# Waits of VectorE and ScalarE in the seven-product stages: for each operation's own data instead of for the engine's last instruction

## The reference

```python
h = _rmsnorm(x, norm1_g) * (1.0 + scale1) + shift1
proj = h @ w_in                       # [1024, 1024] @ [1024, 4352]: queries, keys, values, gates
...
h2 = _rmsnorm(x, norm2_g) * (1.0 + scale2) + shift2
u = h2 @ w_up                         # [1024, 1024] @ [1024, 5632]
a, g = jnp.split(u, 2, axis=-1)
a = ap[:, 0:s] * conv_w[0] + ap[:, 1:s + 1] * conv_w[1] + ap[:, 2:s + 2] * conv_w[2] + conv_b
x = x + gate2 * ((gelu(a) * g) @ w_down)
```

## Time and profile before

| | |
|---|---|
| Median of 3 runs | 2711.78 us (2709.85 to 2713.63) |
| The profiled execution | 2708.78 us, span of its trace 2707.0 us |
| TensorE (PE) busy | 2585.8 us, 96% |
| VectorE (DVE) busy | 1528.0 us, 56%, 2083 instructions |
| ScalarE (ACT) busy | 1104.7 us, 41%, 1865 instructions |
| GpSimd (POOL) busy | 856.5 us, 32%, 627 instructions |
| Mean granted TensorE clock | 0.984 |
| U_IN2's steps on TensorE | from 1325.09 to about 1624 us |
| U_FFN's steps on TensorE | from 2040.29 to about 2449 us |

### The profile page before, as it was taken

One profiled execution on the slowest core, in us unless ns is written; L12 is line 12 of the kernel. 1 busy time (PEld: TensorE's weight loads), 2 busy tenths in 40 slices (PEclk: granted clock), 3 DMA queues, 4 the chain that ended last, 5 costly groups with the idle time before them and its releaser, 6 DMA issues.

```text
span 2707.0 us, 34684 instructions
## 1 busy us (share of the span) xinstructions
PE 2585.8 (96%) x12391; PEld 2150.7 (79%) x12391; DVE 1528.0 (56%) x2083; ACT 1104.7 (41%) x1865; POOL 856.5 (32%) x627
## 2 busy tenths in 40 slices
PE   6999999999899999999899997899997999999998
PEld 3888887888787799987678887778875888887887
DVE  5665755630434566657864437866578777771112
ACT  5200002611410688856544437761365555550000
POOL 2233331032233566630222220243002232324664
PEclk8999999999999999999999999999998999999999
DMA  6344444263365544434253337514342333339833
GB/s 245 99 143 134 146 132 125 86 209 102 133 206 167 129 110 109 110 123 156 76 186 133 109 119 185 181 61 148 89 142 81 109 109 109 109 115 310 287 95 119
DMA packets 377272, 374.81 MB, mean 138 GB/s; under 512 B 36323, under 2 KB 284556, under 8 KB 376972
## 3 DMA queue, kind: packets, MB, share of 16 engines
q1 hardware_dynamic: 346844, 303.91, 37.9%
q10 hardware_dynamic: 30256, 68.69, 6.8%
HBM read 286.55 MB, written 85.98 MB: 138 GB/s over the span
## 4 chain that ended last, share of the span: by engine, by line
PE 74%; DVE 13%; ACT 5%; DMA 3%; issue 2%; SPq 1%; POOL 1%; ACTq 0%; DVEq 0%; POOLq 0%
PE PS L1793 28%; PE PS L1878 20%; PE PS L1947 8%; PE PS L811 5%; PE PS L789 2%; DMA mod_raw<-in_w_ada 1%; PE PS L2018 1%; PE PS L1837 1%; PE PS L775 1%; PE PS L774 1%; DVE opBf L3017 1%; DVE Xr L2998 1%; ACT opBf L2161 1%; PE PS L1860 1%; ACT opA L2165 1%
## 5 line engine op out<-in xcount | busy, mean ns | idle before, releaser
L1793 PE MATMUL PS<-opA,w_hi 128*128 128x512 f32 x2176 | 678.7, 391 | 3.0 <-POOL w_lo L1596 3.0
L1793 PEld LDWEIGHTS PS<-opA,w_hi 128*128 128x128 f32 x2176 | 410.0, 188 | 88.8 <-POOL w_lo L1596 3.4
L1793 PE MATMUL PS<-opA,w_lo 128*128 128x512 f32 x1088 | 424.6, 390 | 0.0
L1591 POOL CAST w_hi<-w_raw 128x1024 fp32r<-128x1024 f32 (+1 forms) x117 | 125.1, 1069 | 784.6 <-PE PS L1793 456.7
L1878 PE MATMUL PS<-opB,Xr 128*128 128x512 f32 x1120 | 309.8, 394 | 15.4 <-ACT M L2341 14.7
L1596 POOL TENSOR_TENSOR w_lo<-w_raw,w_hi 128x1024 fp32r<-128x1024 f32 (+1 forms) x118 | 284.8, 2413 | 35.0 <-ACT w_hi L2220 25.6
L1878 PE MATMUL PS<-opA,Xr 128*128 128x512 f32 x980 | 276.2, 392 | 6.6 <-DVE M L3034 3.0
L1878 PEld LDWEIGHTS PS<-opB,Xr 128*128 128x128 f32 x1120 | 212.8, 190 | 61.9 <-ACT M L2341 16.0
L2676 DVE SCALAR_TENSOR_TENSOR M<-mod_raw,small,M 128x512 f32<-128x512 f32 x168 | 181.0, 1077 | 142.7 <-DMA mod_raw<-in_w_ada 82.2
L1793 PEld LDWEIGHTS PS<-opA,w_lo 128*128 128x128 f32 x1088 | 205.1, 189 | 42.4 <-issue 0.2
L1878 PEld LDWEIGHTS PS<-opA,Xr 128*128 128x128 f32 x980 | 182.2, 188 | 50.7 <-ACT M L2341 8.7
(11 more groups left out here) (266 smaller groups left out, 4757.4 us busy)
## 6 DMA issues: line engine op xcount, KB each, us to landing
mod_raw<-in_w_ada SPq DMA_DIRECT2D x96, 256.0 KB, 2.9
z_dram<-opB ACTq DMA_DIRECT2D x44, 512.0 KB, 3.9
w_raw<-in_a_w_in SPq DMA_DIRECT2D x32, 512.0 KB, 4.6
hin<-q_dram SPq DMA_DIRECT2D x64, 256.0 KB, 6.0
w_raw<-in_w_down SPq DMA_DIRECT2D x32, 512.0 KB, 3.8
opA<-z_dram SPq DMA_DIRECT2D x60, 256.0 KB, 5.2
mod_raw<-in_b_mod_w SPq DMA_DIRECT2D x48, 256.0 KB, 2.8
X<-x_dram SPq DMA_DIRECT2D x24, 512.0 KB, 6.7
```

What stands on the lines that cost most here:

```text
L1591: pool.tensor_copy(hi, raw).then_inc(pool_done, 1)
L1793: ins = pe.matmul(ps, w[:, k0 + k, :], rhs(part, k0 + k), start=(k == 0 and n == 0), stop=(k == chunks - 1 and n == 2))
```

## The change

Three things are changed, all in the two seven-product stages.

1. The waits for the engine's own last instruction go from `weight_high`, `token_high`, `snap`, `in2_copy`, `in2_use`, `first_copies`, `gelu`, `z_high`, `first_tap` on ScalarE and from `weight_low`, `token_low`, `block_sum`, `in2_low`, `first_product`, `z_low`, `gated` and the sums and taps on VectorE. Where an operation reads or overwrites what an earlier one of the same engine wrote or read, and no other wait covers that, it waits for that one by name.
2. `token_sums` takes two chunks at a time: P5 for both, P7 for both, P6 for both, P4 for both. It is called for chunks 0 and 1 at the start of the entry and for 2 and 3 after weight_low P5; the calls after weight_low P4 and P3 go.
3. `other_taps`, both taps of one half in a row, becomes `tap(f, hf, back)`, one tap. For f = 0 and 1 the first taps of both halves come before the second ones. In the steady steps weight_low(q, i + 1, P1) stands between the two taps of (f - 1, 1), and weight_low(q, i + 1, P6) between those of (f, 0).

Matmuls, transfers, GpSimd's and SyncE's queues, and ScalarE's order are not touched.

```diff
@@ ScalarE @@
             def snap(q, i, n):
...
                     elif in2_kind(u) == "parts":
                         act.wait_ge(dve_done, at("in2_lo", u))
+                    else:
+                        act.wait_ge(act_done, at("in2_used", u))
                 if q == U_IN2 and i == 0:
                     act.wait_ge(rstd_out, at("rstd_out"))
-                act.wait_ge(act_done, now(act_done))
...
             def in2_use(i, row):
...
-                act.wait_ge(act_done, now(act_done))
+                if i < 0:
+                    act.wait_ge(act_done, at("in2_copy", u))
...
             def first_tap(f, hf):
...
                     act.wait_ge(dve_done, at("fl", f - 1, hf))
-                act.wait_ge(act_done, now(act_done))
+                if f < 2:
+                    act.wait_ge(act_done, at("fa", f, hf))
@@ VectorE @@
             def token_low(q, which, c):
 
                 dve.wait_ge(act_done, at("token_hi", q, which, c))
-                dve.wait_ge(dve_done, now(dve_done))
...
-            def token_sums(q, c):
...
+            def token_sums(q, c0):
+
+                for which, last in ((P5, None), (P7, P5), (P6, P7), (P4, P6)):
+                    for c in (c0, c0 + 1):
...
+                        if last is None:
+                            dve.wait_ge(dve_done, at("lo", NORM_OF[q], 2 * KC - 1))
+                        else:
+                            dve.wait_ge(dve_done, at("token_sum", q, last, c))
+                        dve.tensor_tensor(out_of, in0, in1, ALU.subtract).then_inc(dve_done, 1)
+                        step(dve_done, "token_sum", q, which, c)
...
             def block_sum(q, i, row, hf):
...
+                    if in2_kind(u) == "parts":
+                        dve.wait_ge(dve_done, at("in2_lo", u))
+                elif row == 0:
+                    dve.wait_ge(dve_done, at("fconv", i + 1, 1))
+                elif i:
+                    dve.wait_ge(dve_done, at("fz", i + 1, hf))
+                if (row, hf) == (1, 0):
+                    dve.wait_ge(dve_done, at("block", q, i, 1, 1))
...
-                dve.wait_ge(dve_done, now(dve_done))
...
-            def other_taps(f, hf):
+            def tap(f, hf, back):
...
+                if back == 1:
+                    dve.wait_ge(act_done, at("ft", f, hf))
+                else:
+                    dve.wait_ge(dve_done, at("tap", f, hf))
...
             def gated(f, hf):
 
                 dve.wait_ge(act_done, at("fg", f, hf))
-                dve.wait_ge(dve_done, now(dve_done))
+                dve.wait_ge(dve_done, at("block", U_FFN, f - 2, 1, hf))
...
                 if i:
-                    other_taps(f - 1, 1)
+                    tap(f - 1, 1, 1)
                     weight_low(q, i + 1, P1)
+                    tap(f - 1, 1, 2)
                     weight_low(q, i, P3)
                     gated(f - 1, 1)
                     block_sum(q, i, 0, 0)
                     z_low(f - 1, 1)
                     weight_low(q, i + 1, P2)
-                    other_taps(f, 0)
+                    tap(f, 0, 1)
                     weight_low(q, i + 1, P6)
+                    tap(f, 0, 2)
                     weight_low(q, i + 1, P5)
                     block_sum(q, i, 1, 1)
```

## The result

The changed kernel takes 2681.35 us, the median of 4 runs (2679.75 to 2681.72), beside 2710.99 us (2709.85 to 2713.63, 4 runs) of the kernel before on the same chip: ratio 0.9885, 95% interval 0.9873 to 0.9897. The forecast was 2692 us, with a range from 2684 to 2705. The direction was right, the gain was 29.6 us where the sum gave 19.8, and the time lies 2.7 us under the range. The profiled execution has a span of 2677.9 us, before 2707.0.

A forecast was written before the change was run, and what follows sets the result against it. TensorE bounds the steady parts, VectorE's queue the two entries. Gains of 9.6, 9.8 and 1.2 us sum to 20.6, less 0.8 for hops 19.8: from 2711.78 to 2692 us, range 2684 to 2705.

The forecast's parts named there:

- first entry, up to P6 of i = 1: First stage's entry: TensorE starts 4.8 us earlier, P3's and P6's gaps shrink 1.4 each, shorter slow stretch 0.4.
- its slow stretch behind: First stage, behind the 2.3 us gap before P6 of i = 1: lowered clock over 10 us, 1.6 us regained.
- The own wait's price: Both stages: VectorE loses 0.12 to 0.20 us per ready instruction; steps become 0.60, ScalarE's copies 0.52 instead of 0.75.
- Rival 2: Both entries: own waits cost nothing, only the order counts; 6 us gain, 2706 us, chance 0.10.
- GpSimd keeps its turn: Both entries: beside GpSimd's weight sums, VectorE instructions with two SBUF inputs still take 1.70 us each.
- rival 3: Both entries: VectorE without gaps keeps GpSimd out, seven contended instructions cost 0.60 instead of 1.70; 2684 us, chance 0.13.
- The sign of being wrong that the prediction named: In GpSimd's queue: its sums growing longer and late would show the forecast wrong; no size given.
- Steady part: Second stage's steady sevens: TensorE busy 316.61 of 317 us, so 0.4 us to win.
- The end: End of the second stage: 0.8 us won of TensorE's 2.75 us idle, bounds 0 and 2.75.
- The second entry: Second stage's entry: P6 of i = 1 comes 10.3 us earlier, less 0.5, so 9.8; an 8.9 us gap stays.
- Taps apart: Second stage's steady sevens: second tap starts about 0.8 us later, but its chain stays hidden with 0.8 us to spare.
- rival 5: Second stage's steady sevens: second tap's chain meets GpSimd's sums, 1.4 us too long in each of 19; 2719 us, chance 0.05.

The follow-up runs named there:

- GpSimd later: Changed kernel with GpSimd's weight sums of the last stage's second product set begun only behind the first conv chunk's last tap: 2673.29 us, ratio 0.9860.

## Why the prediction came out too high

Both profiles, stretch by stretch (predicted, measured):

| stretch | predicted | measured | from |
|---|---|---|---|
| first entry, up to P6 of i = 1 | 8.0 | 13.7 | quad's end to that P6: 40.05 before, 26.38 after |
| its slow stretch behind | 1.6 | 1.6 | that P6 to the first attention product's wait: 267.47, 265.88 |
| second entry, up to P6 of i = 1 | 9.8 | 10.2 | quad's end to that P6: 46.12 (2036.88 to 2083.00), 35.93 (2024.78 to 2060.71) |
| steady sevens of the second stage | 0.4 | 3.9 | P6 to the last P6: 2432.17 - 2083.00 = 349.17; 2406.00 - 2060.71 = 345.29 |
| end of the second stage | 0.8 | 2.4 | last P6 to the next stage: 16.47, 14.06 |

Together 31.7 us before rounding, where the prediction has 20.6; 2.6 us go the other way outside the stretches of the table (the first entry's quad ends 1.7 us later in this execution, at 1318.06 instead of 1316.38, and the first attention waits 0.8 us longer for its transfers), and the spans differ by 29.1. Over all the profiled executions here, in which TensorE's instructions up to that point are the same, the quad ends between 1312.24 and 1320.37 us. What moves it was not tested; it is why the traces are compared stretch by stretch.

- **The own wait's price: right.** Steps of 0.60 and 0.52 as taken from the earlier trace rows. Rival 2, that own waits cost nothing, is dead: order alone gives 2736 us. On the Trainium skill's sentence (VectorE: DVE Perf Modes, The DRAIN you can't avoid), that the semaphore costs nothing extra, row and run disagree with it here: eight equal low parts, each waiting for ScalarE's copy, take 4.90 us without the own wait and 6.26 with it, and a token sum's step is 0.60 us instead of 0.72. The Trainium skill's figure is for eight copies with a semaphore after each or only after the last; what is taken away here is the wait on it.
- **GpSimd keeps its turn: the step that failed.** "I take 1.70, the row of the same pair" held for the first run of sums (1301.89: 8.01 us for eight, with 8.1 in the sum) and for the second stage's taps (6.56 us for four). It failed for the second run of the first entry, where GpSimd began in the middle of VectorE's stream: 0.60 for every instruction, three of which the sum had charged with 1.1 us more ("two instructions caught by the second GpSimd run 2.2" and "one contended instruction"). GpSimd held back by hand in the kernel before takes 3.8 us off the same gap. That is rival 3's mechanism, at one of its two places; its 2684 us, the nearest to the result, counted on all seven contended instructions at both. In the second stage GpSimd got its turn as assumed, but right behind a pause of VectorE of 0.23 us ahead of the taps, of which the prediction says nothing; that it was the pause is read from the traces, not tested there. The sign of being wrong that the prediction named, GpSimd's sums longer and late, came about in the first entry, and with it the kernel became faster, not slower. The start of TensorE came 8.3 us closer to the quad instead of 4.8; with no gap there was hardly a slow stretch either, 5.71 us instead of 8.12 for P1, where I had 0.4 for it. P3's gap fell by 0.6 (1.4 foretold), that of P6 by 2.3 (1.4).
- **Steady part: the term of 0.4 was mis-sized, 3.9.** I took the idle time that a view shows for all that can be won. TensorE before the change:

```profile
2388.00 5.60 PE L1878 MATMUL PS<-opA,w_first 128*128 128x512 f32 x24
...
2407.20 5.60 PE L1878 MATMUL PS<-opA,w_first 128*128 128x512 f32 x24
```

  And in the changed kernel:

```profile
2381.52 5.60 PE L1878 MATMUL PS<-opA,w_first 128*128 128x512 f32 x24
...
2400.56 5.60 PE L1878 MATMUL PS<-opA,w_first 128*128 128x512 f32 x24
```

  No idle time is shown between the first two, yet they are 19.20 us apart, and the second two 19.04. A matmul's record here lasts 0.39 us while the next starts 0.227 later, so a stall of up to 0.16 us hides in the record, and a longer one shows only its excess. In the first step, the starts are 0.14 us late in all, at the first two matmuls of P7, the product that has to wait for snap(q, i, 1). The same instructions in the old order with new waits step by 19.04 us (one of 17 by 19.15), so it was the own waits that made the stalls.
- **The end: 0.8 foretold, 2.4 measured,** within its bounds of 0 and 2.75. The wait of 2.57 us for the snap ahead of the last P7 is gone.
- **The second entry: right,** gap by gap, GpSimd's contention with the taps included, with the luck of that pause: whether GpSimd gets in was called unknown there, and 1.70 us an instruction was the bound that came true.
- **Taps apart: "hidden" was right** for the new waits (the runs with the taps together show no difference), and a ring in rival 5's place was real under the old ones. What I had not seen is that the two parts of the change depend on each other: waits alone 0.9910, order alone 1.0090, both 0.9885.

## What to carry to other kernels

Price an own wait at each of an engine's instructions, not only on the path of today: here it cost 0.12 to 0.20 us an instruction on VectorE and 0.23 on ScalarE, and 23 us in all. An order can be judged only together with its waits; the same order lost 23 us under one set and gained some 7 under the other. To find small stalls of a busy TensorE, measure from one product's start to the same product's start a step later, and compare with a step known to be clean.

## What the hardware showed beyond that

A stream of VectorE instructions with two SBUF inputs and no pause kept one GpSimd operation waiting for 16.81 us (5.74 and 7.64 us in another place). Four times such an operation ended 1.1 to 1.2 us after VectorE's first pause:

| run | VectorE's pause begins | length | GpSimd's operation ends |
|---|---|---|---|
| changed kernel, first entry | 1328.57 | 0.05 | 1329.71 |
| changed kernel, second entry | 2022.02 | 0.23 | 2023.17 |
| own wait at the token low parts | 1318.03 | 0.11 | 1319.19 |
| GpSimd later, its second operation | 2038.98 | 1.50 | 2040.13 |

The 5.74 us operation ended without a pause, 1.24 us after the start of a VectorE instruction that reads one input from PSUM; that this is what let it in was not tested.

Once a VectorE instruction had had to wait for GpSimd, the two took turns, at 1.70 us for a VectorE instruction, pause or none (8.01 us for eight sums of which three were contended, 6.56 for four taps). So in these traces a stream without pauses kept GpSimd out only as long as none of its own instructions had had to wait for GpSimd. Why turns go on in the one case and don't start in the other isn't settled by these runs.
